# The prompt's attention cut into three groups, two of them moved into the gather loop; the sample attention issued in even pieces

## The reference

```
xn = rmsnorm(x);  z = xn @ W_in
conv branch:  GLU -> causal depthwise conv, width 31 -> LayerNorm -> swish      (512 wide)
hgrn branch:  gated linear recurrence, 4 heads of 128 x 128 state               (512 wide)
fox branch:   attention, 8 heads of 64, logit bias = sum of log forget gates    (512 wide)
    prompt: causal, over the prompt's own keys;  sample: over 8 pages of cache and its own keys
m = sum over branches of sigmoid(gate) * (branch @ W_branch);   h = x + m @ W_out
PEER: q = rmsnorm(h) @ wq; 128 + 128 scores for each of 8 heads; top 16 -> 128 experts a token
y = rmsnorm(h + sum over the 128 experts of gelu(u_e . xn) * w_e * v_e)
```

## Time and profile before

| from, to (us of the span) | what runs | us |
|---|---|---|
| 0 to 497 | norm and hgrn | 497 |
| 497 to 984 | fox | 487 |
| 984 to 1225 | trunk of group 0, its C, M and L units | 241 |
| 1225 to 1419 | its output, norm and query parts; choice of tile 0 | 194 |
| 1419 to 2371 | gather loop to slot 308, with the trunk of group 1 | 952 |
| 2371 to 2863 | gather loop, slots 308 to 412, with the sample attention | 492 |
| 2863 to 3763 | gather loop to slot 707, with the trunk of group 2 | 900 |
| 3763 to 4761 | gather loop to the end | 998 |

### The profile page before, as it was taken

One profiled execution on the slowest core, in us unless ns is written; L12 is line 12 of the kernel. 1 busy time (PEld: TensorE's weight loads), 2 busy tenths in 40 slices (PEclk: granted clock), 3 DMA queues, 4 the chain that ended last, 5 costly groups with the idle time before them and its releaser, 6 DMA issues.

```text
span 4761.4 us, 53894 instructions
## 1 busy us (share of the span) xinstructions
PE 3708.2 (78%) x19049; PEld 2813.8 (59%) x19049; DVE 2660.2 (56%) x5621; ACT 2261.7 (48%) x4152; POOL 1400.3 (29%) x1160
## 2 busy tenths in 40 slices
PE   7998799999958888768667778788767666766666
PEld 5666577755735555655455656556655555555555
DVE  3666233344157975564455437966653586756754
ACT  3222111111115565566443445566575566666665
POOL 0000000000003333333443323433333355655644
PEclk9999899999979999888665569999878766666666
DMA  2000100032339999999987889999999999999998
GB/s 76 27 27 27 51 23 23 10 102 95 120 110 415 419 398 414 381 392 404 371 319 251 306 305 382 408 417 414 371 414 376 388 405 421 421 419 420 416 413 341
DMA packets 278736, 1367.53 MB, mean 287 GB/s; under 512 B 33671, under 2 KB 89415, under 8 KB 138213
## 3 DMA queue, kind: packets, MB, share of 16 engines
q0 software_dynamic: 158720, 1143.02, 58.9%
q1 hardware_dynamic: 119789, 221.64, 13.3%
HBM read 1335.23 MB, written 29.69 MB: 287 GB/s over the span
## 4 chain that ended last, share of the span: by engine, by line
DMA 31%; PE 25%; DVE 11%; ACT 7%; issue 3%; POOL 1%; SPq 1%; another core or an unknown queue 0%; DVEq 0%; ACTq 0%; POOLq 0%
DMA p_ring<-in_peer_uv,p_idx 25%; PE psum L1709 8%; DVE p_ring L1777 6%; PE psum L1085 4%; DMA t_w<-in_w_query 4%; PE psum L1164 4%; ACT p_ring L1743 3%; PE psum L1582 2%; PE psum L1089 2%; DMA group<-in_x_all 2%; PE psum L1130 1%; DVE group L1314 1%; ACT p_act_w L1740 1%; POOL p_ring L1689 1%; PE psum L1092 1%
## 5 line engine op out<-in xcount | busy, mean ns | idle before, releaser
L1709 PE MATMUL psum<-ident,p_ring 128*128 128x128 f32 x8704 | 1528.6, 334 | 829.5 <-ACT p_ring L1743 812.0
L1689 POOL DMA_INDIRECT p_ring<-in_peer_uv,p_idx x1088 | 1324.4, 1217 | 2309.9 <-PE psum L1709 1802.6
L1709 PEld LDWEIGHTS psum<-ident,p_ring 128*128 128x128 f32 x8704 | 1262.2, 174 | 1183.1 <-ACT p_ring L1743 1073.9
L1777 DVE CUSTOM_DVE_ANT_0 p_ring<-p_ring,p_xn 128x1024 f32<-128x1024 f32 x1088 | 1329.1, 1223 | 967.2 <-DMA p_ring<-in_peer_uv,p_idx 956.2
L1743 ACT ACTIVATE p_ring<-p_ring,p_act_w 128x1024 f32<-128x1024 f32 x1088 | 1249.6, 1149 | 35.5
L1738 ACT ACTIVATE p_gl<-p_hid 128x1 f32<-128x1 f32 x1088 | 218.8, 201 | 1181.1 <-DVE p_hid L1777 1168.4
L1085 PE MATMUL psum<-group,t_w 128*128 128x384 f32 (+1 forms) x1344 | 452.5, 477 | 8.1 <-DMA t_w<-in_w_conv 8.1
L1164 PE MATMUL psum<-group,t_w 128*128 128x384 f32 (+1 forms) x768 | 280.5, 501 | 87.9 <-DMA t_w<-in_w_query 86.7
L1740 ACT ACTIVATE p_act_w<-p_gl,p_w 128x1 f32<-128x1 f32 x1088 | 320.5, 295 | 35.3
L1085 PEld LDWEIGHTS psum<-group,t_w 128*128 128x128 f32 x1344 | 247.7, 195 | 131.0 <-DMA t_w<-in_w_conv 8.3
L1674 POOL MEMSET c_mean_w<- 128x128 f32 x1 | 0.2, 204 | 946.8 <-POOLq L86 946.8
(11 more groups left out here) (289 smaller groups left out, 3786.2 us busy)
## 6 DMA issues: line engine op xcount, KB each, us to landing
t_w<-in_w_merge SPq DMA_DIRECT2D x72, 768.0 KB
t_w<-in_w_query SPq DMA_DIRECT2D x48, 576.0 KB
p_ring<-in_peer_uv,p_idx POOLq DMA_INDIRECT x1088
group<-in_cache_kT SPq DMA_DIRECT2D x64, 256.0 KB
group<-in_cache_v SPq DMA_DIRECT2D x64, 256.0 KB
t_w<-in_w_conv SPq DMA_DIRECT2D x24, 512.0 KB
t_w<-in_w_outs SPq DMA_DIRECT2D x24, 512.0 KB
h_w<-in_w_hgrn SPq DMA_DIRECT2D x16, 512.0 KB
```

The lines of the kernel that those rows point to most:

```text
L1689: pool.indirect_dma_start(ring[:, at % RING, :], None, io["peer_uv"], bass.IndirectOffsetOnAxis(ap=idx[:, u, c:c + 1], axis=0)).then_inc(r ...
L1709: last = pe.matmul(acc[u][:, k * P:(k + 1) * P], ring[:, at % RING, D + k * P:D + (k + 1) * P], ident[:, :], start=(c == 0 and k % 4 == 0) ...
L1777: dve.tensor_tensor_reduce(out=ring[:, g, 0:D], in0=ring[:, g, 0:D], in1=xn[:, u, :], scale=1.0, scalar=0.0, op0=ALU.mult, op1=ALU.add, ac ...
```

## The change

`stage_fox` is taken out. The attention of the prompt becomes three generators' worth of work inside `stage_experts`, one for each group, described by a `FoxPlan`: group 0 before the loop (slots from -900, its trunk from -880 beside it), group 1 in slots 0 to 100 with its trunk moved to slots 100 to 303, group 2 (tiles 6 and 7 only) in slots 427 to 519 with its trunk moved to slots 519 to 707. The slots for a unit of the two later trunks are cut to fit. The fox weights are loaded again for groups 1 and 2 (12 chunks each, through `wst`), the keys, values and bias rows of the earlier groups are written to device memory and read back. There is one score buffer instead of two, and both copies of the transposed shares are made by ACT. The trunk of group 0 uses the four PSUM banks that the loop's accumulators use later, so that it can run beside group 0's attention. M units now take the hgrn products of all eight column blocks first, then the fox products, then the conv products. The sample attention keeps its 13 slots a sequence; its scores, values and page loads are issued one small piece a slot.

The diff, cut to its core:

```diff
-STAGES = (stage_norm, stage_hgrn, stage_fox, stage_experts)
+STAGES = (stage_norm, stage_hgrn, stage_experts)
...
-        self.parts = [(dc, nb) for dc in range(KD) for nb in (1, 2)] + [(dc, 0) for dc in range(KD)]
+        self.parts = [(dc, nb) for nb in (1, 2, 0) for dc in range(KD)]
...
-START = -600
-PLANS = (Plan(0, START, 10, 8, 20, 5, 4), Plan(1, 0, 7, 5, 22, 5, 4), Plan(2, 417, 6, 5, 20, 5, 4))
-SAMPLE, BATCH = 308, 13
-CHOOSE = {3: 37, 6: 65}
+class FoxPlan:
+    def __init__(self, g, start, proj, step):
+        self.g, self.start, self.proj, self.step = g, start, proj, step
+        self.tiles = 3 if g < 2 else 2
+        self.full, self.off, self.units = self.tiles * P, g * GW, 2 * self.tiles
+        self.twice = step < 3
+        self.first = 24 * g
+        self.pair = proj + 2 + step * (self.units - 1) + 3
+        self.end = start + 4 * self.pair + 8
+    def at(self, i):
+        return self.start + i * self.pair
+    def score(self, i, n):
+        return self.at(i) + self.proj + 2 + self.step * n
...
+START = -900
+BATCH = 13
+FOX0, FOX1 = FoxPlan(0, START, 10, 2), FoxPlan(1, 0, 8, 2)
+PLAN0, PLAN1 = Plan(0, START + 20, 10, 8, 20, 5, 4), Plan(1, FOX1.end, 4, 3, 12, 3, 3)
+SAMPLE = PLAN1.end + 6
+FOX2 = FoxPlan(2, SAMPLE + DB * BATCH + 14, 7, 3)
+FOXES, PLANS = (FOX0, FOX1, FOX2), (PLAN0, PLAN1, Plan(2, FOX2.end, 4, 3, 11, 3, 2))
+CHOOSE = {3: PLAN1.end - 253, 6: PLANS[2].end - 637}
...
+        def fox_sp(sp, plan):
...
+                sp.dma_start(cg[:, :], io["cs_scratch"][:, off:end]).then_inc(fc_loaded, 16)
+                for hh in range(2):
+                    sp.dma_start(kf[hh][other[hh], :], io["kbias_scratch"][other[hh], 0:end]).then_inc(fc_loaded, 16)
...
+                    for u in range(3):
+                        yield from weights(sp, BASES[g] + 3 * i + u, io["w_fox"][rows(3 * i + u), :], KD * P, plan.at(i) - 7)
+                    yield plan.at(i) + 5
+                    sp.wait_ge(fpv, after(plan.unit(i, 0)))
+                    for hh in range(2):
+                        sp.dma_start(kf[hh][own[hh], 0:off], io["kT_scratch"][i * P + hh * 64:i * P + hh * 64 + 64, 0:off]).then_inc(fk_loaded, 16)
+                    sp.dma_start(vf[:, 0:3 * g, :], io["v_scratch"].rearrange("(t p) c -> p t c", p=P)[:, 0:3 * g, rows(i)]).then_inc(fvl_loaded, 16)
...
+        def fox_pe(pe, plan):
+            bank, wide = pb, m.psum[:, 2048:3072]
+            def scores(i, n):
...
+                pe.wait_ge(fexp, after(u))
+                for part in range(t // 4 + 1):
+                    wd = min(512, keys - part * 512)
+                    pe.matmul(wide[:, part * 512:part * 512 + wd], qf[hh][:, j * P:(j + 1) * P], kf[hh][:, part * 512:part * 512 + wd],
+                              start=True, stop=(part < t // 4), skip_group_check=True)
...
+            for i in range(4):
+                for n in range(plan.units + 2):
+                    at = plan.score(i, n)
+                    yield at
...
+                    if plan.twice and n >= 2:
+                        turn(i, n - 2, 1)
+                    if n < plan.units:
+                        scores(i, n)
+                    if plan.twice:
+                        yield at + 1
+                        if 1 <= n <= plan.units:
+                            turn(i, n - 1, 0)
+                        if n >= 2:
+                            values(i, n - 2)
+                    elif 1 <= n <= plan.units:
+                        turn(i, n - 1, 0)
+                        yield at + 1
+                        turn(i, n - 1, 1)
+                        yield at + 2
+                        values(i, n - 1)
...
+        def fox_act(act, plan):
+            def softmax(i, n):
+                act.wait_ge(fmax, after(u + 1))
...
+                act.activation(pf[x][:, 0:(t + 1) * P], wide[:, 0:(t + 1) * P], ACT.Exp, bias=fnmax[:, x:x + 1],
+                               accum_out=frsum[:, x:x + 1]).then_inc(fexp, 1)
...
+                    if plan.twice:
+                        yield at
+                        if 1 <= n <= plan.units:
+                            softmax(i, n - 1)
+                        if n >= 2:
+                            turned(i, n - 2, 0)
+                            yield at + 1
+                            turned(i, n - 2, 1)
...
+            if g == 2:                                       # trunk_sp
                 for i in range(2):
-                    yield plan.start - 6
+                    yield plan.start - 2
+                    sp.wait_ge(fo_ok, after(32))
...
         def sample_sp(sp):
-                yield SAMPLE + BATCH * b - 7
+                yield SAMPLE + BATCH * b - 4
...
                 for n in range(PAGES):
+                    yield SAMPLE + BATCH * b - 4 + n // 2
...
         def sample_pe(pe):
                 for part, (off, n) in enumerate(CHUNKS):
-                    if part:
-                        yield at + 3 * part
+                    yield at + 5 * part
...
-                        if part < 2 and x % 2 == 1:
-                            yield at + 3 * part + (x + 1) // 2
+                        if part < 2:
+                            yield at + 5 * part + 1 + x
+                            pe.wait_ge(k_loaded[part], 16 * 4 * (b + 1))
...
+        def sample_values(pe):
+                at = SAMPLE + BATCH * b + 15
...
                 for x in range(4):
-                    if x:
-                        yield at + 15 + x
                     for n in range(9):
+                        if n in (0, 4):
+                            yield at + 2 * x + n // 4
```

More of the change, by code:

```diff
@@ L961, in product_made, with weights, released @@
                 eng.wait_ge(glu_ok, after(4 * plan.g + unit.n + 1))
+        def weights(sp, k, src, width, due):
+            yield due
+            if k >= 3:
+                released(sp, k - 3)
+            sp.dma_start(wst[k % 3][:, 0:width], src).then_inc(w_loaded[k % 3], 16)
+        def released(sp, k):
+            g = sum(k >= x for x in BASES[1:])
+            il = k - FIRST[g]
+            if il < 0:
+                i, v = divmod(il + FOX, 3)
+                sp.wait_ge((fq_z, fk_z, fv_z)[v], after(4 * g + i + 1))
+            elif il < 32:
+                unit, second = owner(PLANS[g], il)
+                if unit.kind == "C" and not second:
+                    sp.wait_ge(g_z, after(28 * g + unit.z + 1))
+                else:
+                    sp.wait_ge(v_z, after(28 * g + unit.z + 1))
+            elif il < 40:
+                sp.wait_ge(o_ps, after(8 * g + il - 31))
+            else:
+                sp.wait_ge(s_ps, after(16 * g + il - 39))
@@ new lines, in owner, with fox_begins @@
+        def owner(of, il):
+            for unit in of.filled:
+                first = chunk_of(of, unit) - FIRST[of.g]
+                if first <= il < first + (2 if unit.kind == "C" else 1):
+                    return unit, il > first
+        def fox_begins(eng, plan):
+            g = plan.g
+            if g:
+                eng.wait_ge(s_ok, after(16 * g))
+                eng.wait_ge(q_ok, after(16 * g))
+            if g == 2:
+                eng.wait_ge(exp_ok, after(DB))
+                eng.wait_ge(tb_ok, after(DB))
+                eng.wait_ge(tn_ok, after(DB))
+                eng.wait_ge(o_ok, after(8 * DB))
@@ L1006, in trunk_sp @@
                     dc, nb = plan.parts[unit.n]
-                    yield from weights(k, io["w_merge"][(3 * dc + nb) * P:(3 * dc + nb + 1) * P, :], 12 * P, unit.slot - 8)
+                    yield from weights(sp, k, io["w_merge"][(3 * dc + nb) * P:(3 * dc + nb + 1) * P, :], 12 * P, unit.slot - 8)
             if g == 2:
@@ L1198, in units_act @@
                     act.wait_ge(var_ps, after(g + 1))
[L1199 removed]
+                    act.activation(std[g][:, 0:n], banks[g][unit.gate][:, 0:n], ACT.Sqrt, bias=keep["eps"][:, 0:1]).then_inc(std_ok, 1)
         def swish_act(act, plan):
```

758 lines of the change are left out of this document (431 added, 327 removed).

## The result

The changed kernel takes 4624.7 us (median of 4 runs, 4619.95 to 4631.82), the kernel before 4752.7 (median of 4): a ratio of 0.9726, 95% interval 0.9696 to 0.9755. That is 128 us less where 64 were forecast: inside the range and on the forecast side, at twice the size.

A forecast was written before the change was run, and what follows sets the result against it. TensorE was taken to bound the part before the loop, DMA the loop. A gain of 310 us less 248 lost in the loop made 62, so 4690 us from 4754; own range 4600 to 4770, with rivals 4500 to 4860.

The forecast's parts named there:

- the first part: Prompt work before the loop: group 0's attention beside its trunk takes 175 us instead of 487, a gain of 312.
- the attention stages: Attention of groups 1 and 2 in the loop: ScalarE's Exps with table loads set the pace, 360 and 330 us.
- The sign I gave: Group 1's attention, slots 0 to 100: ScalarE above 90% busy, two table loads around each of 24 Exps.
- the trunks: Trunks of groups 1 and 2 in fewer slots: 705 and 685 us, TensorE near 95% and DMA below 95%.
- the weights come late: Rival, 20%: query weights in the later trunks arrive 16 us after issue, 168 us more, giving 4860 us.
- The loop absorbs it: Rival, 24%: TensorE's slack takes the moved work, the loop grows by 50 to 150 us, median 4430 to 4600.
- the tables' second load: Rival, 3%: a table switch costs at most a second load's length, 102 us more in all, giving 4792 us.
- the uneven sample: Rival, 3%: even pieces even nothing out in the sample attention, 4.8 us a slot, 47 us more, 4737 us.
- the sample attention: Sample attention with values in halves: 4.35 us a slot, so 104 slots take 452 us instead of 497.
- the end of 3.4: Lower end for the sample attention: 3.4 us a slot, set by DMA transfers at 406 GB/s.
- the part that the sum gave 45: Even pieces of the sample attention: 104 slots in 452 us instead of 497, a gain of 45 us.
- The sign set for this stage: Sample attention: stage near 450 us, with no wait of GpSimd above 4 us.

## Why the prediction was right in direction and half in size

**Right: the first part.** 312 us of gain were summed, 325 came. The first trunk matmul of group 0 starts at 554.76 where the sum had 553. The four units ahead of it take 12 us (10 in the sum, half of them uncovered); from there to 900 TensorE is busy 343.8 of 345.2 us, so the longer softmax chains, for which 15 were allowed, do not show. That is most of the 13 us by which the gain was larger.

**Right: the attention stages, for the reason given.** 360 and 330 forecast, 357 and 337 measured, the load at 1.28 us without a drain behind it. Counted by ScalarE's row scalings, the twelve slots with units of a pair took 3.9 us each in group 1 and the other eleven 3.1, where the sum had 3.9 and 3.0; in group 2 4.4 and 2.9, where it had 4.2 and 3.0. The sign I gave, ScalarE above 90% busy over the stage, was wrong (75%) and did not follow from my own sum, which has it busy for some 82%. In the slots with units of group 1's last pair it is full, and in those of group 2 it is not, since there it waits for TensorE:

```profile
1393.00:1423.00 30.00, 24.07 (x154) 19.43 (x153) 19.95 (x52) 29.19 (x48) 10.32 (x8) 0.94 0.97 391
2907.00:2948.00 41.00, 30.01 (x182) 24.23 (x181) 16.68 (x31) 28.70 (x46) 8.66 (x9) 0.87 0.77 285
```

That the loads are the cause was shown by taking them out, that the re-reading is not by leaving part of it out.

**Nearly right in size, wrong in reason: the trunks.** 705 and 685 forecast, 720 and 659 measured, which is in part luck. I called them bound by TensorE near 95% and the DMAs below; the rows have TensorE at 83% and 83.5% and the DMAs at 0.94 and 0.95. Group 2's conv slots were summed as VectorE's work with 5% lost, 232 us; they took 215. A query chunk there took 8.7 us for the 10 forecast, in group 1 11.0 for 11.5.

**Refuted: the weights come late.** What TensorE waited for query weights in the changed kernel (waits: us in total, times, longest):

```profile
PE psum L1388 <- DMA t_w<-in_w_query: 60.2, 16, 10.5
```

In the kernel before it was 86.7 us in 15 waits. In the changed kernel these loads landed in a median of 10.0 us in group 1's query part and 7.7 in group 2's. The 13.05 and 15.96 of the earlier trace rows are single loads that held up the chain, and the trace before has no median, so whether they land sooner now is not known. *The loop absorbs it* fails too, with 193 us lost in the loop where its time needed 50 to 150 (its lower end of 4430 does not follow from these; they give 4494); the tables' second load and the uneven sample did not come about.

**The step that failed: the sample attention.** The term is the slot time of 4.35 us there, made of 4.6 in eight slots of 13 and 3.3 in the rest; it measured 3.87. The 4.6 us were TensorE's durations, taken from the uneven stage at its granted 0.62 as if they were the operations' own. One slot of the even stage in the changed kernel (timeline of TensorE: transposes, the bias part of the scores, values of a half, new values):

```profile
2452.89 1.09 PE L1947 MATMUL psum<-ident,p_ring 128*128 128x128 f32 x8
2453.91 1.12 PE L1781 MATMUL psum<-t_tmp,group 64*128 64x512 f32 x2
2454.96 1.07 PE L1817 MATMUL psum<-group 128*128 128x16 f32 x8
2455.95 0.39 PE L1817 MATMUL psum<-group,v_new 64*128 64x16 f32 x2
```

Transposes take 1.09 us instead of 1.97 and half a head pair's values 1.07 instead of 1.72, and the slot lasts 3.39 us (2452.89 to 2456.28). The eight slots with values of one sequence, and the five behind them (windows, columns as above):

```profile
2391.80:2418.10 26.30, 25.31 (x152) 16.87 (x152) 15.45 (x24) 15.83 (x27) 14.35 (x12) 1.00 1.01 408
2418.10:2442.08 23.98, 13.92 (x76) 9.79 (x75) 13.17 (x28) 13.29 (x22) 10.83 (x10) 0.71 0.84 283
```

So a slot with values takes 3.3 us, at a granted 1.00 (2.4 GHz throughout), with TensorE busy for 25.3 of 26.3 us and the DMA engines full; that is the end of 3.4 that I had named for the transfers. The other five take 4.8 where I had 3.3: there VectorE waits for the last values and ScalarE runs the Exp. Over the stage it is 3.4 for the 56 slots with values and 4.6 for the 48 without. The two errors go opposite ways, so that the miss is smaller than the 4.6 alone would have made it: 104 slots take 402 us, not 452. VectorE's waits for values and scores, 151 us of the old stage, had no place in the sum at all. I also put the gain of the spread requests at nothing: bunched again they cost 46 us. Taken together the spreading is worth 76 us alone and 94 in place, the move 35: of the 128 us the larger part comes from the part that the sum gave 45. The sign set for this stage, no wait of GpSimd above 4 us, failed as well: one for the ring reached 12.1 us and one for the gates' buffer 16.5, in a stage at a DMA share of 0.95.

## What to carry to other kernels

A duration read in a stage holds for that stage's mix: when a change spreads or bunches work, price its operations from a stage that already looks as it will, and keep the old figure as one end only. Count requests as well as instructions, and look at the queue that they share: eight small requests in one go, ahead of the gathers in GpSimd's queue, are the likeliest reason why bunched requests cost more here than bunched products. Ask of every wait in an engine's fixed order what stands behind it; here it was the dot products. Where two engines take turns in a fixed order, a busy share below 80% over a stage does not mean that there is room: ask which operation lies between one engine's end and the other's start, and remember that moving an operation which ends a wait moves the wait.

## What the chip showed that was not expected

A reciprocal over a wide row takes 6.4 ns a column on VectorE (4953 ns for 768), where scaling and adding takes 0.73 (560 ns). The Trainium skill (VectorE: DVE Perf Modes, section Walkthrough: the 8-slice pipeline in each mode) says that the reciprocal is an iterative division with a repeat count of 8. These rows show 8.8 times the time of a scaling pass; no run here shows that the repeat is the reason.

The stage of the sample attention is as long at a granted 0.64 as at 0.73 (493 us both, with the old scores and with the even ones), so here the mean clock of the stage is no measure of its time.
